# New tokens' latents as one more split page: a 128-row single-pass product in place of the whole fp32 product in paged attention

## The reference

```python
def mla_sample(q_nope, q_pe, latent_new, k_pe_new, cache_lat, cache_kpe, page_table, layer, w_ukv, k_nope_norm):
...
    def one(args):
        pages, qn, qp, lat_new, kp_new = args
        lat = jnp.concatenate([cache_lat[layer, pages].reshape(past, KV_LORA).astype(lat_new.dtype), lat_new], axis=0)
        kp = jnp.concatenate([cache_kpe[layer, pages].reshape(past, QK_ROPE).astype(kp_new.dtype), kp_new], axis=0)
        k_nope, v = expand_kv(lat, w_ukv, k_nope_norm)
        return attend(qn, qp, k_nope, kp, v, mask)
```

## Time and profile before

| what | value |
|---|---|
| runs of the kernel | 1660.06, 1664.48, 1664.24 us; median 1664.24 |
| profiled execution: span | 1656.5 us, 34705 instructions |
| median less the profile's span | 7.7 us |
| PE busy | 1596.1 us (96%), 10896 matmuls |
| DVE, ACT, POOL busy | 1060.0, 895.3, 464.8 us |
| granted TensorE clock | 0.9 or more of full speed in all 40 slices of the span |
| pages stage | from 159 to 423 us of the span, and again from 984 us |

### The profile page before, as it was taken

The page is one execution under the profiler, slowest core; times in us unless marked ns, Lnnn a source line. Parts: engine busy times, 40 slices in busy tenths (PEclk is TensorE's granted clock), DMA queues, the critical chain, the costliest instruction groups (busy, mean ns, idle before and its releaser), DMA issues.

```text
span 1656.5 us, 34705 instructions
## 1 busy us (share of the span) xinstructions
PE 1596.1 (96%) x10896; PEld 1530.2 (92%) x10896; DVE 1060.0 (64%) x1625; ACT 895.3 (54%) x1616; POOL 464.8 (28%) x533
## 2 busy tenths in 40 slices
PE   7898999999999999999989989999999999999999
PEld 6776999999999999999978779999999999999999
DVE  6566777778644676664374757777785447666633
ACT  5586666666534454443346856666665345444432
POOL 1133366766620010000012323666666200000000
PEclk9999999999999999999999989999999999999999
DMA  6322354444444444444444213645445445444443
GB/s 237 115 75 74 121 186 146 154 146 142 142 147 138 157 153 150 152 149 146 138 154 131 85 43 122 186 150 157 144 131 157 140 137 161 147 150 152 147 146 119
DMA packets 114515, 233.07 MB, mean 141 GB/s; under 512 B 12881, under 2 KB 78482, under 8 KB 114258
## 3 DMA queue, kind: packets, MB, share of 16 engines
q1 hardware_dynamic: 111890, 222.94, 42.6%
q0 software_dynamic: 2496, 8.55, 1.5%
HBM read 228.98 MB, written 2.46 MB: 140 GB/s over the span
## 4 chain that ended last, share of the span: by engine, by line
PE 79%; DVE 5%; issue 4%; ACT 3%; POOLq 3%; DVEq 2%; POOL 1%; ACTq 1%; DMA 0%; SPq 0%
PE PS L739 48%; PE PS L981 21%; PE PS L1014 1%; PE PS L1015 1%; PE PS L976 1%; POOLq L660 1%; POOL r_lo L680 1%; DVEq L1767 1%; POOLq L658 1%; POOLq L672 1%; ACT w_hi L1235 1%; PE PS L764 1%; DVE xc L1769 1%; PE PS L920 1%; ACTq L1239 0%
## 5 line engine op out<-in xcount | busy, mean ns | idle before, releaser
L1684 DVE TENSOR_TENSOR w_lo<-raw,w_hi 128x1024 fp32r<-128x1024 f32 x258 | 317.0, 1229 | 263.0 <-ACT w_hi L1235 249.8
L1235 ACT ACTIVATE w_hi<-raw 128x1024 fp32r<-128x1024 f32 x258 | 273.1, 1060 | 337.0 <-PE PS L739 312.9
L739 PE MATMUL PS<-h_hi,w_hi 128*128 128x320 f32 x1360 | 426.4, 314 | 13.9 <-DVE h_lo L1687 8.3
L739 PE MATMUL PS<-h_hi,w_lo 128*128 128x320 f32 x1360 | 421.3, 310 | 0.0
L739 PE MATMUL PS<-h_lo,w_hi 128*128 128x320 f32 x1360 | 421.3, 310 | 0.0
L739 PEld LDWEIGHTS PS<-h_hi,w_hi 128*128 128x128 f32 x1360 | 256.3, 188 | 20.1 <-DVE h_lo L1687 9.6
L739 PEld LDWEIGHTS PS<-h_lo,w_hi 128*128 128x128 f32 x1360 | 256.5, 189 | 0.6
L739 PEld LDWEIGHTS PS<-h_hi,w_lo 128*128 128x128 f32 x1360 | 256.3, 188 | 0.0
L1235 ACT ACTIVATE ksqp<-PS 128x512 f32<-128x512 f32 x256 | 153.2, 598 | 170.8 <-PE PS L981 167.7
L981 PE MATMUL PS<-comb_hi,lt_hi 128*128 128x288 f32 x1024 | 239.7, 315 | 0.0
L2045 DVE TENSOR_REDUCE kss<-ksqp 128x8 f32<-128x512 f32 x256 | 173.2, 680 | 91.0 <-ACT ksqp L1235 90.6
(11 more groups left out here) (304 smaller groups left out, 2639.2 us busy)
## 6 DMA issues: line engine op xcount, KB each, us to landing
raw<-in_stream SPq DMA_DIRECT2D x258, 512.0 KB, 3.5
tpage<-in_tcache SPq DMA_DIRECT2D x256, 192.0 KB, 2.5
rrow<-in_rcache SPq DMA_DIRECT2D x256, 128.0 KB, 2.6
x<-in_xT SPq DMA_DIRECT2D x2, 640.0 KB, 5.4
sbias<-in_sbias POOLq DMA_DIRECT2D x2, 640.0 KB, 5.7
out_yT<-x SPq DMA_DIRECT2D x4, 320.0 KB, 2.2
const<-in_consts SPq DMA_DIRECT2D x1, 1088.0 KB
wgate<-in_wgate POOLq DMA_DIRECT2D x2, 512.0 KB, 3.9
```

Source lines behind the costliest of these rows:

```text
L739: done = mm(out, w[:, slot, c], a, start=first and n == 0 and m == 0, stop=last and n == len(pairs) - 1 and m == 2)
L1235: return nc.scalar.activation(out, in_, func, **kw)
L1684: V.tensor_tensor(w_lo[:, s, :], raw[:, s, :], f(w_hi[:, s, :]), ALU.subtract).then_inc(lo_done.sem, 1)
```

## The change

1. `latnew` is made on 128 partitions in fp32r: rows 0 to 63 the high halves of the new latents, rows 64 to 127 the low ones. PE writes the transposed latents a second time to the other 64 partitions of bank 1 (two more matmuls), ACT rounds all 128 rows and writes a further pair of columns (zeros), DVE subtracts (`lo(low, ...)`, a new 64x256 operation behind the rotary split), and DVE, not ACT, then releases bank 1.
2. `snew` is copied by DVE to partitions 64 to 127 (64x512), between the last `masked_max` of the prompt attention and the split of `y2`.
3. `snp` has 128 rows; ACT does one more exponential per sequence (`snp_hl[:, 0:64]`, rounded to fp32r) ahead of the old one.
4. POOL gets one subtraction per sequence (128x64, the low half) between the cast and the subtraction of the first quarter of probabilities, and every quarter's signal `p_split` now comes from a drain behind the subtraction instead of from the subtraction itself.
5. The product of line 1011 becomes one fp32r matmul with 128 rows, 128 columns of `snp_hl` and 258 of `latnew`.

```diff
--- before.py
+++ after.py
@@ -114,8 +114,8 @@
     comb_lo = sb("comb_lo", [128, 2, 2, 320], f32r, on=st)
     qabs = sb("qabs", [128, 2, NB, HT], on=st)
     q128 = sb("q128", [128, NB, HT], f32r, on=st)
-    latnew = sb("latnew", [TS, KVL + 2], on=st)
-    snew = sb("snew", [TS, NB, HT], on=st)
+    latnew = sb("latnew", [128, KVL + 2], f32r, on=st)
+    snew = sb("snew", [128, NB, HT], on=st)
     wv = sb("wv", [128, 2, H * DV], on=st)
 
     st2 = ExitStack()
@@ -159,7 +159,11 @@
     olatT = sb("olatT", [128, 2, H, TS], on=st4)
     olat = sb("olat", [128, KVL + 2], on=st4)
     m1 = sb("m1", [128, HT], on=st4)
-    snp = sb("snp", [TS, HT], on=st4)
+    before_low = ExitStack()
+    beside_low = sb("beside_low", [128, HT], on=before_low)
+    snp = sb("snp", [128, HT], on=before_low)
+    before_low.close()
+    snp_hl = sb("snp_hl", [128, 2 * HT], f32r, on=st4)
     mx = sb("mx", [HT, 1 + HT + 2], on=st4)
     linv = sb("linv", [128, 2], on=st4)
     beside_kpe = sb("beside_kpe", [128, 121], on=st4)
@@ -310,10 +314,10 @@
     q128_hi = Signal("rotary_spread_hi", 1)
     q128_ready = Signal("rotary_spread_ready", 1)
     latT_mm = Signal("new_latent_transposed", 1)
-    latnew_ready = Signal("new_latent_ready", 1)
+    latnew_ready = Signal("new_latent_ready", 2)
     sn_mm = Signal("new_scores_done", 1)
     sn_copied = Signal("new_scores_copied", 1)
-    sn_ready = Signal("new_scores_masked", 1)
+    sn_ready = Signal("new_scores_masked", 2)
     ps_mm = Signal("prompt_scores", H)
     ps_max = Signal("prompt_max", H)
     ps_exp = Signal("prompt_exp", H)
@@ -626,10 +630,10 @@
             pool.wait_ge(sn_copied.sem, sn_copied.at(l, 1))
             pool.sem_inc(waits_passed, 1)
             pat = [[8, NB], [0, H], [1, NT]]
-            nc.gpsimd.affine_select(out=snew[:], in_=snew[:], compare_op=ALU.is_ge, fill=MASKED, base=0,
+            nc.gpsimd.affine_select(out=snew[0:TS], in_=snew[0:TS], compare_op=ALU.is_ge, fill=MASKED, base=0,
                                     pattern=pat, channel_multiplier=-1)
             pool.drain()
-            nc.gpsimd.affine_select(out=snew[:], in_=snew[:], compare_op=ALU.is_ge, fill=MASKED, base=0,
+            nc.gpsimd.affine_select(out=snew[0:TS], in_=snew[0:TS], compare_op=ALU.is_ge, fill=MASKED, base=0,
                                                 pattern=[[-8, NB], [0, H], [0, NT]], channel_multiplier=1).then_inc(sn_ready.sem, 1)
             pool.wait_ge(abs_ready.sem, abs_ready.at(l, 1))
             pool.sem_inc(waits_passed, 1)
@@ -670,7 +674,10 @@
                 at, src = slice(4 * (k % 2), 4 * (k % 2) + 4), prob[:, 4 * k:4 * k + 4, :]
                 nc.gpsimd.tensor_copy(p_hl[:, at, 0:HT], src)
                 pool.drain()
-                nc.gpsimd.tensor_tensor(p_hl[:, at, HT:2 * HT], src, f(p_hl[:, at, 0:HT]), ALU.subtract).then_inc(p_split.sem, 1)
+                if k == 0:
+                    nc.gpsimd.tensor_tensor(snp_hl[:, HT:2 * HT], snp[:], f(snp_hl[:, 0:HT]), ALU.subtract)
+                nc.gpsimd.tensor_tensor(p_hl[:, at, HT:2 * HT], src, f(p_hl[:, at, 0:HT]), ALU.subtract)
+                pool.drain().then_inc(p_split.sem, 1)
 
             def rows_lo(q, m):
 
@@ -880,7 +887,8 @@
             pe.wait_ge(bank_free[1].sem, banks.take(l, 1))
             pe.sem_inc(waits_passed, 1)
             for k in range(2):
-                last = nc.tensor.transpose(PS[0:TS, 1, 128 * k:128 * k + 128], lat[:, k, SEQ:T], cst("ident"))
+                nc.tensor.transpose(PS[0:TS, 1, 128 * k:128 * k + 128], lat[:, k, SEQ:T], cst("ident"))
+                last = mm(PS[TS:2 * TS, 1, 128 * k:128 * k + 128], lat[:, k, SEQ:T], cst("ident"), start=True, stop=True)
             last.then_inc(latT_mm.sem, 1)
 
             pe.wait_ge(kT_ready.sem, kT_ready.at(l, 1))
@@ -1008,7 +1016,7 @@
                 pe.wait_ge(s_exp.sem, s_exp.at(l, q + 1))
                 pe.sem_inc(waits_passed, 1)
                 mm(PS[:, 7, 0:ROW], w, r_hi[:, r, :], start=True, stop=False)
-                mm(PS[0:HT, 7, 0:ROW], snp[:], latnew[:], start=False, stop=False)
+                mm(PS[:, 7, 0:ROW], snp_hl[:], latnew[:], start=False, stop=False)
                 last = mm(PS[:, 7, 0:KVL], w, r_lo[:, r, :], start=False, stop=False)
             else:
                 mm(PS[:, 7, 0:KVL], w, r_lo[:, r, :], start=False, stop=False)
@@ -1062,8 +1070,8 @@
 
             for b in (0, 1, 2, 3, 4, 6, 7):
                 pe.wait_ge(bank_free[b].sem, banks.last(l, b))
-            pe.wait_ge(sn_ready.sem, sn_ready.at(l, 1))
-            pe.wait_ge(latnew_ready.sem, latnew_ready.at(l, 1))
+            pe.wait_ge(sn_ready.sem, sn_ready.at(l, 2))
+            pe.wait_ge(latnew_ready.sem, latnew_ready.at(l, 2))
             pe.wait_ge(q128_ready.sem, q128_ready.at(l, 1))
             sequence(l, 0, 0, tail=False, values=False, older=False)
             pe.wait_ge(bank_free[5].sem, banks.last(l, 5))
@@ -1442,9 +1450,9 @@
                          PS[:, 6, :].rearrange("p (h j b t) -> p h j b t", h=4, j=2, b=NB)[:, :, jt], ACT.Copy)
             last.then_inc(q128_hi.sem, 1)
             act.wait_ge(latT_mm.sem, latT_mm.at(l, 1))
-            A(latnew[:, 0:KVL], PS[0:TS, 1, 0:KVL], ACT.Copy)
-            A(latnew[:, KVL:], ones[0:TS, 0:2], ACT.Copy)
-            release(1)
+            A(latnew[:, 0:KVL], PS[:, 1, 0:KVL], ACT.Copy)
+            A(latnew[0:TS, KVL:], ones[0:TS, 0:2], ACT.Copy)
+            A(latnew[TS:2 * TS, KVL:], ones[TS:2 * TS, 0:2], ACT.Copy, scale=0.0)
             act.drain().then_inc(latnew_ready.sem, 1)
             act.wait_ge(sgu_scaled.sem, sgu_scaled.at(l, 1))
             for j in range(4):
@@ -1520,6 +1528,7 @@
             if not (isinstance(b, int) and b == 0):
                 act.wait_ge(p_split.sem, p_split.at(l, b * 4))
             A(prob[:], nope(par), ACT.Exp, scale=SCALE)
+            A(snp_hl[:, 0:HT], snp[:], ACT.Exp, scale=SCALE)
             A(snp[:], snp[:], ACT.Exp, scale=SCALE).then_inc(s_exp.sem, 1)
 
         def sequence(l, b, par, tail=True, last=False):
@@ -1902,6 +1911,10 @@
                     last = V.tensor_tensor(dst, src, f(dst), ALU.subtract)
             last.then_inc(q128_ready.sem, 1)
             release(6)
+            dve.wait_ge(latnew_ready.sem, latnew_ready.at(l, 1))
+            low = latnew[TS:2 * TS, 0:KVL]
+            lo(low, PS[TS:2 * TS, 1, 0:KVL], low).then_inc(latnew_ready.sem, 1)
+            release(1)
 
         def spatial_sums(l):
             dve.wait_ge(sgu_mm.sem, sgu_mm.at(l, 4))
@@ -1931,7 +1944,7 @@
             masked_max(0)
             masked_max(1)
             dve.wait_ge(sn_mm.sem, sn_mm.at(l, 1))
-            V.tensor_copy(snew[:].rearrange("p b (h t) -> p h b t", h=H),
+            V.tensor_copy(snew[0:TS].rearrange("p b (h t) -> p h b t", h=H),
                                        PS[0:TS, 2, :].rearrange("p (h b t) -> p h b t", h=H, b=NB)).then_inc(sn_copied.sem, 1)
             release(2)
             def normalised(h):
@@ -1959,6 +1972,8 @@
             pages_lo(l, 0, 0)
             normalised(5)
             masked_max(7)
+            dve.wait_ge(sn_ready.sem, sn_ready.at(l, 1))
+            V.tensor_copy(snew[TS:2 * TS], snew[0:TS]).then_inc(sn_ready.sem, 1)
             dve.wait_ge(y2h.sem, y2h.at(l, 1))
             lo(y2_lo[:], va[:], y2_hi[:]).then_inc(y2_ready.sem, 1)
             normalised(6)
@@ -2000,7 +2015,7 @@
             dve.drain()
             V.tensor_reduce(m1[:], mxh[:].rearrange("p a c -> p c a"), AX.X, ALU.max)
             dve.drain()
-            V.tensor_tensor(m1[0:TS, :], m1[0:TS, :], of_seq(snew, b), ALU.max).then_inc(s_m1.sem, 1)
+            V.tensor_tensor(m1[0:TS, :], m1[0:TS, :], of_seq(snew, b)[0:TS], ALU.max).then_inc(s_m1.sem, 1)
 
         def row_max(l, b, par):
             dve.wait_ge(s_m1T.sem, s_m1T.at(l, b + 1))
@@ -2014,7 +2029,7 @@
             V.tensor_tensor(nope(par), nope(par), over(mb, NPG), ALU.subtract)
             if not (isinstance(b, int) and b == 0):
                 dve.wait_ge(pv_mm.sem, pv_mm.at(l, b * NPG + (1 - NPG)))
-            V.tensor_tensor(snp[:], of_seq(snew, b), mb[0:TS], ALU.subtract).then_inc(s_sub.sem, 1)
+            V.tensor_tensor(snp[:], of_seq(snew, b), mb, ALU.subtract).then_inc(s_sub.sem, 1)
 
         def copy_values(l, b):
             dve.wait_ge(pv_mm.sem, pv_mm.at(l, b * NPG + NPG))
```

## The result

| | before | changed |
|---|---|---|
| median of 6 runs | 1664.26 us | 1676.40 us |
| range of the runs | 1660.06 to 1665.3 | 1670.88 to 1681.7 |
| ratio, 95% interval | | 1.0083 (1.0065 to 1.0100) |
| span of the profiled execution | 1656.5 us | 1680.2 us |
| mean granted clock in it | 0.993 | 0.983 |

The account below looks back on a forecast made before the run. PE is busy 96% of the span but waits for POOL's `lt_hi` behind the burst, so POOL's chain bounds there. 4.8 + 1.8 + 0.4 + 0.8 + 0.3 - 2.6 = +5.5 us on 1664.24 gives 1669.7 us, range 1662.5 to 1675.5.

Parts of the forecast that it names:

- The product, 0.66 us a burst: PE's burst, line 1010 to 1014: three steps take 0.35 us in place of 1.01, at most 10.6 us saved.
- Saved in the tail, 2.6 us: Four bursts of q = 6 and 7 among the gate products, where PE is the bound: 4 x 0.66 us saved.
- Nothing saved in b = 2 to 6: Ten bursts with PE waiting for POOL right behind: a shorter burst only makes the wait longer, 0 us.
- The second rival: PE keeps its saving in all 16 bursts: -9.5 us, 1654.7 us, faster; 4 in 100.
- POOL's chain, 0.6 for b = 3 to 6: Added subtraction and drain lengthen POOL's chain behind the burst by 0.6 us in 8 sequences: +4.8 us.
- The sequences b = 2: ACT's exponential, POOL's growth and the third quarter's drain cost 0.9 us in each of two layers: +1.8 us.
- The sequences b = 7: POOL's rows come 0.7 us later against 0.7 of slack before page 4: 2 x 0.2 = +0.4 us.
- The other three drains ... covered: POOL's other drains delay it some 0.35 us each, covered by its waits for ACT's high rows: 0 us.
- The third rival: Every drain shows: second and fourth quarters cost 12 sequences 0.3 us each, +3.6, 1673.3 us, slower; 11 in 100.
- My own sign of being wrong: Wrong if page 4's wait stays under 1.2 us, b = 3 to 6 pages shorten, or another page start waits.
- The front, +0.8: DVE's copy of `snew` ahead of the last prompt probabilities, for which PE waits: 0.4 us in each of two layers.
- The two rivals that kept the time the same or faster: POOL's chain does not grow, 1662.7 us, 15 in 100; PE keeps its saving everywhere, 1654.7 us, 4 in 100.

Follow-up runs that it names:

- e4: Kernel before, with only the drain ahead of POOL's signal added in all four quarters; 1666.06 us, ratio 1.0018.
- e9: Only the front of the change, with a whole fp32 product over the 128 packed rows and nothing added to POOL or ScalarE in the sequences; 1664.57 us, ratio 0.9998.
- e12: Kernel before, with only TensorE's spatial products moved ahead of head 0's transposes; 1654.53 us, ratio 0.9943.
- e1: Changed kernel, with the drain ahead of the signal kept only in the first quarter; 1674.98 us, ratio 1.0062.
- e2: Changed kernel, with seven extra unread matmuls on PE behind the burst of sequences 2 to 6; 1670.02 us, ratio 1.0048.
- e3: Changed kernel, with the low half of the new tokens' probabilities subtracted by VectorE instead of POOL, and no drains before the signal; 1658.15 us, ratio 0.9968.
- e10: Changed kernel, with TensorE's spatial products moved ahead of head 0's transposes; 1670.48 us, ratio 1.0048.
- e8: Changed kernel, with the new tokens' product again a whole fp32 product on the same 128 packed rows; 1669.33 us, ratio 1.0033.
- e5: Changed kernel, with POOL's queries for the next sequence done one chunk later; 1656.51 us, ratio 0.9960.

## Why the prediction was half right

Right in direction and in mechanism up to the wait, wrong in what follows the wait.

- **The product, 0.66 us a burst:** 1.01 to 0.37, confirmed. Saved in the tail, 2.6 us: the last key page to the end of the span is 410.7 us before, 410.9 to 411.1 in e4, e9 and e12, and 409.4 to 409.8 in the changed kernel, e1, e2, e3 and e10. That is some 1.3 a layer, the added 0.3 for ACT's exponential already off it. PE's wait at line 1029 grew with it, from 1.3 to 1.64 us in each layer.
- **Nothing saved in b = 2 to 6:** confirmed by the wait, 1.77 us where I forecast 1.7, and 18.0 in all where I wrote "over 18". The second rival, that PE keeps its saving, did not happen.
- **POOL's chain, 0.6 for b = 3 to 6:** the burst page of e8, undisturbed by the clock, grew by 0.46 to 0.64 us, 4.4 in all (forecast 4.8). The sequences b = 2 grew by 1.1, both layers together (forecast 1.8): page 12, where I had put 0.33 for the third quarter's drain, starts only 0.04 to 0.06 later behind page 11, and the burst page grew by 0.27. The sequences b = 7 grew by 0.3 to 0.4 together (forecast 0.4).
- **"The other three drains ... covered":** wrong for the fourth quarter. The third rival named the second and the fourth, in 12 sequences; only the fourth showed, in 6 (b = 3 to 5). It cost 2.1 to 2.3 us (changed kernel and e8), forecast 0 and in the rival 3.6. I had judged the slack at a page start by the 0.27 us between `lt_hi` and page 4. Page 0 has more waits ahead of it: in the changed kernel `lt_hi` ends at 294.25 and page 0 starts at 294.89, 0.64 later, so what looked like slack was not. My own sign of being wrong, another page start that begins to wait, is this one.
- **The front, +0.8:** e9 shows -0.3 (-3.2 to +2.5); the runs cannot tell 0.8 from 0. The wait itself, for the last heads' probabilities, grew from 2.01 to 2.59 us in each layer, where I had 0.4.
- **The failed step** is "a shorter burst only makes the wait longer: nothing saved". It took idle time of PE as free. It cost 1.5 us each time that the clock fell behind it: 10.7 us in the profiled execution, and, as an estimate for the runs, at 16 of 24, the rate of the three kernels with such gaps, 8 x 0.67 x 1.5 = 8 us.

Together, with the sizes measured: 7.6 (e2's growth in b = 2 to 6, page 0 in it) + 0.3 (b = 7) - 2.6 (tail) + 8 (clock) = 13.3 us, against 13.8 (10.8 to 16.6) from the ratio. Not in this sum is the tail: its wait of 1.62 to 1.64 us was followed by the half clock in 4 of 12 cases in the six profiles that have it (both of e8's, one each in e10 and e5), some 1 us more by the same price. Without the clock it is 5.3, which is what I had forecast, 5.5, partly by luck: page 0 was missing and b = 2 too dear. The two rivals that kept the time the same or faster had 19 in 100 between them; no case of mine had the clock, though the earlier trace rows gave the wait and my own text its growth to 1.7 us. And the trace before held the warning. The table ahead of the prediction says 0.9 or more of the full clock in all 40 slices; the page has an 8 in the 24th, 952 to 994 us:

```profile
PEclk9999999999999999999999989999999999999999
```

In that slice, in the second layer, PE waits for the first head's probabilities,

```profile
954.03 0.54 PE L947 MATMUL PS<-const,sp_ 128*128 128x128 f32 x3 [1.77 <-DVE sp_ L1943]
```

and from 955.6 to 962.4 the granted clock is 0.50: the idle time that I forecast behind the burst, with what follows it. Behind two more waits in that layer, of 1.79 us (to 896.4) and 2.01 us (to 978.3), it was 0.50 for 3.4 us as well.

The rule of the Trainium skill on the lock between DVE and POOL that the prediction cites (SBUF — State Buffer, Who interferes with whom) held: in b = 4 the casts began at 300.84, DVE's `lt_lo` ran from 300.89 to 301.62, and the casts took 0.88.

## What to carry to other kernels

Taking work from an engine that waits right behind it is not neutral: it lengthens the idle stretch, and on TensorE work after that stretch may run at half speed. Before shortening a burst on TensorE, add the saving and the growth of the releaser's chain to the idle time in the trace, and look whether stretches of that length elsewhere in the same trace are followed by a lower granted clock. Look for them by narrow windows: a fall of 3.4 us is 4% off the mean of a slice of 41 us and does not show in the page's digit. If such stretches are there, shorten the releaser's chain first (here: one subtraction to VectorE, queries one chunk later) or move independent work into the gap; and read a clock drop from several profiles before it is charged to a change.
